# RWKV-7 and windowed attention block on one core: centred value tokens, row-tiled small products, unit product folded into the scores

## The reference, cut to what matters

```python
z = h @ w_in                                   # r, k, v, decay/rate/gate inputs, q, k, v, gates
w_log = -softplus(-(w0 + tanh(zw) @ w2)) - 0.5 # decay product, inner dimension 64
a = sigmoid(a0 + za @ a2)                      # rate product, inner dimension 64
# per head: S = S * w + (S aa) bb + v k ;  y = S r      (16 heads of 64)
mean = mean(y, axis=-1); var = mean(square(y - mean), axis=-1)
y = (y - mean) * rsqrt(var + GN_EPS) * lnx_w + lnx_b + bonus * v
s = q @ keys * 64 ** -0.5                      # chunks of 64 queries, 128 keys, softmax with a sink
```

## Time and profile before

| | |
|---|---|
| runs | 1233.83, 1238.17, 1239.98 us; median 1238.17 |
| profiled execution, own time | 1233.64 us |
| its span | 1232.0 us |
| mean granted TensorE clock | 0.988 |
| TensorE busy | 1147.1 us (93%) |
| VectorE, ScalarE, GpSimd busy | 655.6, 541.2, 92.3 us |
| weights loaded by SyncE's queue | 79.98 MB |

### The profile page before, as it was taken

How to read it: one execution, slowest core, us unless ns; L and a number is a source line. 1 busy time by engine, 2 the same in 40 slices (tenths; PEclk the granted TensorE clock), 3 DMA queues, 4 the chain that set the end, 5 groups by cost and what they waited for, 6 DMA issues and landing times. The chain is left out here.

```text
span 1232.0 us, 18748 instructions
## 1 busy us (share of the span) xinstructions
PE 1147.1 (93%) x7023; PEld 923.8 (75%) x7023; DVE 655.6 (53%) x1089; ACT 541.2 (44%) x991; POOL 92.3 (7%) x148
## 2 busy tenths in 40 slices
PE   4998999997989989999898799997999999999996
PEld 4887888885767767777677588885888888888785
DVE  4223545556667666676776444426566556553323
ACT  4435545554353443524544334335555464542222
POOL 8000000111011011010111001010000000000000
PEclk9999999999999999999999999998999999999998
DMA  8432232321011010110312245341323333322321
GB/s 209 103 86 86 60 103 78 90 82 35 10 53 44 10 53 9 44 44 10 104 40 71 74 134 156 112 125 57 95 86 101 98 89 97 90 88 86 91 81 73
DMA packets 171780, 97.23 MB, mean 79 GB/s; under 512 B 30873, under 2 KB 166727, under 8 KB 171719
## 3 DMA queue, kind: packets, MB, share of 16 engines
q1 hardware_dynamic: 166192, 79.98, 23.0%
q0 software_dynamic: 5376, 16.37, 4.4%
q10 hardware_dynamic: 151, 0.04, 0.0%
HBM read 87.98 MB, written 8.39 MB: 78 GB/s over the span
## 5 line engine op out<-in xcount | busy, mean ns | idle before, releaser
L1041 DVE TENSOR_TENSOR wlo<-raw,whi 128x1024 fp32r<-128x1024 f32 x148 | 181.2, 1225 | 335.0 <-ACT whi L667 335.0
L667 ACT ACTIVATE whi<-raw 128x1024 fp32r<-128x1024 f32 x148 | 156.2, 1057 | 264.0 <-PE ps L1533 262.8
L1528 PE MATMUL ps<-xnh,whi 128*128 128x512 f32 x352 | 140.4, 399 | 4.0 <-DVE xnl L1427 4.0
L1533 PE MATMUL ps<-xnh,wlo 128*128 128x512 f32 x352 | 139.6, 397 | 0.0
L1530 PE MATMUL ps<-xnl,whi 128*128 128x512 f32 x352 | 139.6, 397 | 0.0
L1528 PE MATMUL ps<-xh,whi 128*128 128x512 f32 x304 | 122.8, 404 | 0.0
L1533 PE MATMUL ps<-xh,wlo 128*128 128x512 f32 x304 | 120.2, 395 | 0.0
L1530 PE MATMUL ps<-xl,whi 128*128 128x512 f32 x304 | 120.1, 395 | 0.0
L1528 PEld LDWEIGHTS ps<-xnh,whi 128*128 128x128 f32 x352 | 66.5, 189 | 22.9 <-DVE xnl L1427 4.5
L1533 PEld LDWEIGHTS ps<-xnh,wlo 128*128 128x128 f32 x352 | 66.5, 189 | 15.9
L1530 PEld LDWEIGHTS ps<-xnl,whi 128*128 128x128 f32 x352 | 66.5, 189 | 15.4
(11 more groups left out here) (323 smaller groups left out, 2300.1 us busy)
## 6 DMA issues: line engine op xcount, KB each, us to landing
raw<-in_w_in SPq DMA_DIRECT2D x108, 256.0 KB, 3.2
raw<-in_w_up SPq DMA_DIRECT2D x88, 256.0 KB, 3.1
raw<-in_w_down SPq DMA_DIRECT2D x32, 256.0 KB, 2.9
gates_scratch<-gst POOLq DMA_DIRECT2D x16, 256.0 KB, 2.3
raw<-in_w_proj_a SPq DMA_DIRECT2D x16, 256.0 KB, 3.0
raw<-in_w_proj_b SPq DMA_DIRECT2D x16, 256.0 KB, 4.3
gl<-gates_scratch POOLq DMA_DIRECT2D x16, 256.0 KB, 3.8
raw<-in_w_out SPq DMA_DIRECT2D x16, 256.0 KB, 3.1
```

What stands on the lines that cost most here:

```text
L667: act.activation(flat(whi[:, hb]), flat(raw[:, b]), ACT.Copy).then_inc(w_hi, 1)
L1041: dve.tensor_tensor(flat(wlo[:, hb]), flat(raw[:, b]), flat(whi[:, hb]).bitcast(F32), ALU.subtract).then_inc(w_lo, 1)
L1528: pe.matmul(ps[bank][:, :], whi[:, hb, k, :], hi(k), start=first and k == 0, stop=False)
L1533: ins = pe.matmul(ps[bank][:, :], wlo[:, hb, k, :], hi(k), start=False, stop=last and k == kn - 1)
```

## The change

- Value tokens: the four transposes of v become four products with `centred` (unit matrix less the mean over each head), placed ahead of those of b and k and waiting for 7 masks instead of 8. `norm_mean` and `centre` go. ScalarE squares the scan's output directly and then copies it with the scale `lw`.
- The norm of the pair before moves: variance sums between the halves of the scores, deviations behind them, `scaled_output` ahead of the value tokens' copy, `with_bonus` at level 3; `gated` stays at level 5.
- Decay and rate products are two row tiles, 64 rows each, into two banks, issued together at the end of level 6 ahead of its filler step; the decay's tanh follows the key norms' copy.
- Attention scores are 8 products of 128 columns on 64 rows, alternating between the row halves and reading `kb` directly; the two `kc` copies per chunk go.
- `gb` gets -1 on its diagonal once, so that n1 carries the unit matrix, and the product with `nident16` in the remainder goes (8 per pair).

The diff, without declarations, semaphore lists and a few setup lines:

```diff
@@ -546,13 +538,13 @@
             diagonal(ident16, 1.0)
-            diagonal(nident16, -1.0)
             chain(pool.memset(eps_col[:, 1:2], 64e-5))
...
                     chain(pool.memset(t[h * HD:(h + 1) * HD, h * HD:(h + 1) * HD], value))
+            chain(pool.tensor_tensor(centred[:, :], ident[:, :], headmean[:, :], ALU.subtract))
@@ -605,9 +597,13 @@
                 attention_out(c)
-            pool.wait_ge(win_in, 8)
+            pool.wait_ge(scores_ps, 16)
             pool.wait_ge(vwin_in, 8)
-            pool.memset(gb[:, :, :, :], 0.0).then_inc(cleared, 1)
+            chain(pool.memset(gb[:, :, :, :], 0.0))
+            own = gb[:, :, :, 0:C].rearrange("p j h t -> p (j h) t")
+            pool.affine_select(out=own, in_=own, compare_op=ALU.not_equal, fill=-1.0, base=0,
+                               pattern=[[0, 2 * NT], [-1, C]], channel_multiplier=1)\
+                .then_inc(cleared, 1)
             for c in (6, 7):
@@ -734,10 +730,7 @@
                 act.activation(qc[:, :, :], q[:, :, bass.ds(c * AC, AC)], ACT.Copy,
-                               scale=HD ** -0.5)
-                act.activation(kc[0:HD, :, 0, :], kb[0:HD, :, bass.ds(c * AC, P)], ACT.Copy)
-                act.activation(kc[HD:P, :, 1, :], kb[HD:P, :, bass.ds(c * AC, P)], ACT.Copy)\
-                    .then_inc(win_in, 1)
+                               scale=HD ** -0.5).then_inc(win_in, 1)
@@ -793,13 +786,11 @@
-            def norm_head(d):
+            def norm_square(d):
                 act.wait_ge(out_ps, d + 1)
-                act.activation(ysb[:, :], ps[6][:, :], ACT.Copy).then_inc(y_copied, 1)
-
-            def norm_square(d):
-                act.wait_ge(yc_ready, d + 1)
-                act.activation(ysq[:, :], ysb[:, :], ACT.Square).then_inc(ysq_ready, 1)
+                act.activation(ysq[:, :], ps[6][:, :], ACT.Square).then_inc(ysq_ready, 1)
+                act.activation(ysb[:, :], ps[6][:, :], ACT.Copy, scale=pcol("lw", d))\
+                    .then_inc(y_scaled, 1)
@@ -853,8 +845,6 @@
                                        ACT.Copy).then_inc(y_ready[0], 1)
-                    if lv == 0 and d is not None:
-                        deviation(d)
                     if lv == 2:
@@ -863,10 +853,9 @@
                         gate_tile(2 * n)
-                    if lv == 5 and following:
-                        decay_tanh(n + 1)
                     if lv == 6 and following:
                         key_norm_back(n + 1)
+                        decay_tanh(n + 1)
                 transposed(LEVELS - 1)
@@ -931,9 +920,9 @@
                         hi_part(ybh, qb, i)
-                norm_head(n - 1)
+                norm_square(n - 1)
+                deviation(n - 1)
                 score_copy(n)
-                norm_square(n - 1)
                 gate_tile(2 * n - 1)
@@ -1082,10 +1070,10 @@
                 mask = notfirst[:, bass.ds(c * AC, P)].unsqueeze(1).to_broadcast([P, 4, P])
-                dve.wait_ge(scores_ps, c + 1)
-                for g in range(2):
-                    last = dve.tensor_tensor(sc[:, 4 * g:4 * g + 4, :],
-                                             ps[2 + g][:, :].rearrange("p (u k) -> p u k", k=P),
+                dve.wait_ge(scores_ps, 2 * c + 2)
+                for half in range(2):
+                    last = dve.tensor_tensor(sc[:, half:8:2, :],
+                                             ps[2 + half][:, :].rearrange("p (u k) -> p u k", k=P),
                                              mask, ALU.add)
@@ -1172,7 +1160,7 @@
                     dve.wait_ge(cleared, 3)
-                dve.wait_ge(tok_ps, n + 1)
+                dve.wait_ge(tok_ps, n * 3 + 1)
                 dve.tensor_copy(vp[:, :, 0:4:3, :],
@@ -1207,11 +1195,6 @@
-            def centre(d):
-                dve.wait_ge(mean_ps, d + 1)
-                dve.tensor_tensor(ysb[:, :], ysb[:, :], ps[4][:, :], ALU.subtract)\
-                    .then_inc(yc_ready, 1)
-
             def add_bonus(d):
@@ -1219,8 +1202,8 @@
                 dve.wait_ge(rstd_ps, d + 1)
-                chain(dve.scalar_tensor_tensor(ysb[:, :], ysb[:, :], pcol("lw", d), ps[4][:, :],
-                                               ALU.mult, ALU.mult))
+                dve.wait_ge(y_scaled, d + 1)
+                chain(dve.tensor_tensor(ysb[:, :], ysb[:, :], ps[4][:, :], ALU.mult))
@@ -1264,12 +1247,14 @@
                             .then_inc(y_ready[1], 1)
-                    if lv == 1 and d is not None:
-                        deviations(d)
+                    if lv == 2 and d is not None:
+                        add_bonus(d)
+                    if lv == 3 and d is not None:
+                        with_bonus(d)
                     if lv == 4 and following:
                         key_norms(n + 1)
-                    if lv >= 2 and lv < 6 and d is not None:
-                        (add_bonus, scaled_output, with_bonus, gated)[lv - 2](d)
+                    if lv == 5 and d is not None:
+                        gated(d)
                     if lv >= 4 and not following:
@@ -1358,17 +1343,17 @@
                     masked(n, f)
-                centre(n - 1)
+                deviations(n - 1)
                 for f in range(4, 8):
...
                 weights(N_GATE + 2 * n)
+                scaled_output(n - 1)
                 value_tokens(n)
...
                              lambda: y_lo(0, 0, 3), lambda: y_lo(0, 1, 4), lambda: y_lo(0, 2, 5)])
-            centre(PAIRS - 1)
             add_bonus(PAIRS - 1)
@@ -1566,13 +1551,14 @@
                 pe.wait_ge(win_in, c + 1)
-                for g in range(2):
-                    for ii in range(2):
-                        t = 4 * g + 2 * ii
-                        ins = pe.matmul(ps[2 + g][:, ii * 2 * P:(ii + 1) * 2 * P],
-                                        flat(qc[:, t:t + 2, :]), flat(kc[:, g, :, :]),
-                                        start=True, stop=True)
-                ins.then_inc(scores_ps, 1)
+                for t in range(0, 8, 2):
+                    for half in range(2):
+                        hs = slice(half * HD, (half + 1) * HD)
+                        ins = pe.matmul(ps[2 + half][:, t // 2 * P:(t // 2 + 1) * P],
+                                        qc[hs, t:t + 2, :].rearrange("p a b -> p (a b)"),
+                                        kb[hs, t // 4, c * AC:c * AC + P], start=True, stop=True)
+                        if t == 6:
+                            ins.then_inc(scores_ps, 1)
@@ -1584,13 +1570,12 @@
-            def decay_lora(n, bank=4):
-                pe.matmul(ps[bank][:, :], lora[:, n * P:(n + 1) * P], lora_w_in[:, :], start=True,
-                          stop=True).then_inc(lora_ps, 1)
-
-            def rate_lora(n, bank=5):
-                pe.matmul(ps[bank][:, :], lora[:, n * P:(n + 1) * P], lora_a_in[:, :], start=True,
-                          stop=True).then_inc(lora_ps, 1)
+            def small_products(n, banks=(4, 5)):
+                cols = slice(n * P, (n + 1) * P)
+                for h in range(2):
+                    hs = slice(h * HD, (h + 1) * HD)
+                    pe.matmul(ps[banks[h]][:, :], lora[hs, cols], lora_in[hs, :], start=True,
+                              stop=True).then_inc(lora_ps, 1)
@@ -1616,11 +1601,6 @@
                 turned(4, ysq).then_inc(rstd_ps, 1)
-
-            def norm_mean(d):
-                pe.wait_ge(y_copied, d + 1)
-                pe.matmul(ps[4][:, :], headmean[:, :], ysb[:, :], start=True, stop=True)\
-                    .then_inc(mean_ps, 1)
@@ -1644,9 +1624,9 @@
                     if f == 4:
+                        if d is not None:
+                            norm_var(d)
                         fill()
-                        if d is not None:
-                            norm_mean(d)
                     if f >= 4:
@@ -1658,11 +1638,16 @@
                 if d is not None:
-                    norm_var(d)
+                    deviations(d)
+                for j in range(NT):
+                    if j == 0:
+                        pe.wait_ge(g_ready, n * 8 + 7)
+                    ins = pe.matmul(ps[2][:, j * P:(j + 1) * P], z[:, n + 16, j * C:(j + 1) * C],
+                                    centred[:, :], start=True, stop=True)
+                ins.then_inc(tok_ps, 1)
                 pe.wait_ge(g_ready, n * 8 + 8)
-                for b, src in ((0, bp), (1, kp), (2, z[:, n + 16, :])):
-                    ins = turned(b, src)
-                ins.then_inc(tok_ps, 1)
+                for b, src in ((0, bp), (1, kp)):
+                    turned(b, src).then_inc(tok_ps, 1)
                 if d is not None:
@@ -1689,14 +1674,10 @@
-                    if lv == 2 and d is not None:
-                        deviations(d)
                     if lv == 3 and following:
...
                         gate(d)
-                    if lv == 5 and following:
-                        decay_lora(n + 1)
```

(37 more changed lines are left out.)

## The result

The changed kernel takes 1218.24 us (median of 4 runs, 1215.41 to 1221.17) against 1238.38 us before, a ratio of 0.984 with a 95% interval of [0.982, 0.987]. The forecast was 1218.0, with a range of 1209 to 1228. Both medians scatter: measured again later (e9), the same two kernels stood 17.9 us apart (1220.25 and 1238.18).

The account below looks back on a forecast made before the run. TensorE, busy 93% of the span, was taken as the bound; in the recurrence only where others wait for it. Terms sum to 21.3 us, less 2 for the clock: 19.3 off 1238.2, forecast 1218, range 1209 to 1228.

Parts of the forecast that it names:

- attention scores: Products of r, k and v: row-tiled scores take 1.07 us against 1.72 per chunk, seven chunks, 4.6 us off.
- decay and rate products ahead of pair 0: Dense part before the recurrence: both as two row tiles take 1.06 us instead of 1.86, 0.8 us off.
- middle pairs, six: Recurrence: each pair 1.9 us shorter, mostly at level 2 (0.95) and level 5 (0.75); 11.4 us off in all.
- pair 0: First pair of the recurrence, no norm work: masks start 0.85 us earlier; with remainder and tokens 1.2 us off.
- pair 7: Last pair of the recurrence, with no next pair: 0.95 + 0.7 + 0.15, 1.8 us off.
- tail: Last pair's serial norm ahead of the second projection: a wait and the mean product go, 1.5 us off.
- clock, and when the first rows land: Recurrence: one or two short falls of TensorE's clock, 2 us lost; the forecast sized no first-load term.
- rival D: More gain: pair 0's clock fall gets shorter and tiling switches cost less, 1209 to 1212 us; chance 0.07.
- rival A: VectorE becomes the bound at a pair's final decay scan and level 0: 4.5 us back, 1221 to 1225; chance 0.15.
- B: Short falls of the clock in most pairs, from a thinner stretch: 10 us back, 1226 to 1231; chance 0.10.
- E: Row tiles of 128 and 512 columns don't run together, in scores and decay/rate products: 1230 us; chance 0.03.
- C: Slower: levels 3 to 5 of seven later pairs fall to 1.2 GHz, 5.2 us each: 1253 us; chance 0.03.

Follow-up runs that it names:

- e9: The changed kernel with no edit, measured again beside the kernel before: 1220.25 us, 0.986 of before.
- e2: The changed kernel with the attention scores alone put back on all 128 rows, keys copied into a zero-padded block: 1220.89 us, 0.987 of before.
- e1: The changed kernel with each chunk's four score products of one row half ahead of the other half's, instead of alternating: 1224.06 us, 0.989 of before.
- e7: The changed kernel with the norm's later steps back at their old places, mean product still removed: 1240.52 us, 1.004 of before.
- e4: The changed kernel with VectorE's bonus add moved back from level 3 to behind the key norms of level 4: 1230.05 us.
- e6: The changed kernel with one more fp16 product per unit in the remainder, against zeros, replacing the removed unit product: 1225.19 us.
- e3: The changed kernel with the decay and rate products alone put back on all 128 rows at their old places: 1214.65 us.
- e5: The changed kernel with two extra VectorE operations of 0.43 us per pair ahead of the decay scan: 1225.07 us.

## Why the prediction was right

The mechanism was as forecast: the period came out, and of its parts the largest, the moves of the norm. That the total was right to 0.3 us is luck. Measured again, the changed kernel took 1220.25, 2.25 over the forecast, and stood 17.9 below the kernel before for the 20.1 of the first time; and errors of both signs lie in the sum. Term by term, measured from the traces and by taking parts back:

| term | forecast | measured | by |
|---|---|---|---|
| attention scores | 4.6 | 2.5 to 2.9 | spacing of chunks, e2 |
| decay and rate products ahead of pair 0 | 0.8 | 0.6 | key sums to key norms |
| middle pairs, six | 11.4 | 11.5 | period |
| pair 0 | 1.2 | 2.0, of which 1.0 to 1.2 is a shorter fall | scores to scan 0, e1 and e2 |
| pair 7 | 1.8 | 2.2 | scan 6 to scan 7 |
| tail | 1.5 | 1.8 | scan 7 to second projection |
| clock, and when the first rows land | -2 | -0.7 and -2.9 in the medians, -8.3 in the profiled pair | the two measurements; the three rises |

The terms but the last make 20.8 us with 2.7 for the scores, forecast 21.3. Against 20.1 and 17.9 between the medians that leaves 0.7 and 2.9 for the clock and the first loads, where 2 was set aside. In the two profiled executions they took 8.3: one pair of executions doesn't give this term.

**Pair 0: the size was there, in part for another reason.** Its fall is 10.2 us long before the change and 6.8 after it. In e1 and e2, which are the changed kernel from there on, it is 10.2 again, and the stretch from the first score product to scan 0 takes 33.3 and 33.1 us for the 34.1 of before. So the change itself gave 0.8 to 1.0 where 1.2 was forecast; the rest came with the shorter fall, which the forecast had only as rival D.

**Scores: mis-sized.** "8 slots of 0.109 and 0.2, so 1.07 us against 1.72: 0.65 less per chunk" took the switch from starts inside a row-tiled group and the start behind it. A switch also holds back the group's first record, which comes 0.20 behind the last transpose instead of 0.11, and the second record behind the group, 0.34 instead of 0.23. The group did take 1.09; the chunk gained 0.41. The same 0.2 is missing in the products ahead of pair 0: 0.6 for 0.8. So the term that was mis-sized is the price of a group's two switches, 0.2 in the prediction and 0.4 in the traces.

**A middle pair: 1.9 forecast, 1.92 measured, in other parts.** Moves of the norm: 0.95 at level 2 and 0.7 at level 5 forecast, 1.65 measured by e7, less its falls (1.73 in the last period, which had none), of it 0.77 for the bonus add by e4. Remainder: 0.25 forecast, 0.47 by e6; ScalarE's copies didn't hold the rest back, and the 0.45 counted in full. Products: "the level could have gone on only at 507.85 ... 0.4" was no gain. With the bonus add gone, the masks wait for the key norms, and the decay product ended under these. At level 6 the row tiles cost more than the 0.1 of the forecast, by the switch again. Together e3 finds a loss of 0.25 in the period. The mean product's removal is the rest: 1.92 - 1.65 - 0.47 + 0.25 leaves 0.05, as forecast, although it was the largest single product taken out. That is what is left over if the parts add up; no run takes this part back alone.

**What would show it.** Period 47.8: yes. Records in pairs: yes, in 1.1 us. Level 2 right behind its filler: yes (494.14 and 494.38, a filler's own distance). The update of level 5 waits 0.67 us, forecast "about 0.8". Clock full from 320 to 660: yes. VectorE's last sums: they still wait 0.3 us for TensorE, so rival A did not decide, by a third of a microsecond. Clearing gb: VectorE's maxima beside the clear take 679 to 691 ns, the last chunk's too, so the cost of 0 stands.

**The rivals.** B's mechanism exists: a middle pair half a microsecond longer, for any reason, showed it in two or three of six pairs (e4, e5, e6) and e7 in all. The forecast argued against it only by the full slices of before; what protects the changed kernel is thin, and the chance of 0.10 was no exaggeration. Why in e4 to e6 some pairs fall and others, with the same instructions, don't is not settled here. One hint: in e7 the six falls start 51.20 us apart, five times alike, while its scans are 50.85 to 51.14 apart, so that they drift from 39.9 to 40.7 us behind the scan. So the starts follow something other than the pair's own time, and when a pair comes may matter as well as what it does; no run tests that. E is out by the records in pairs, and for 512 columns by L1577: its four records start two by two, and the next product follows 1.06 us behind the first. C's size never came: a fall in a middle pair was 3.4 us long and cost 1.6. The half of D on pair 0's fall came, but in the profiled execution falls elsewhere took more than it gave.

## What to carry to other kernels

Cost a row-tiled group by the distance between two fixed points around it, not by its own records: here a pair of switches took 0.4 us, so 8 short products gained 0.41 of an expected 0.65, and the decay and rate products as two row tiles cost a pair 0.25 more than on all rows, where one of them fitted into a wait. Look for the wait first and then for the work: moving two filler steps into waits gave 1.35 us of each period, where the whole change gave 1.92, and kept the clock up besides. See for each wait which engine ended it: one of these two was a table load of ScalarE, not the masks. When a pipeline's pairs are compared, measure the period and list falls of the clock apart; totals of single runs differ by 6 us for the same period, and the gain between two medians was once 20.1 and once 17.9.

## What was not expected of the hardware

- A switch between full-height matmuls and row tiles costs 0.2 us in each direction, since neither side loads weights under the other: starts 0.20 and 0.34 us apart where 0.11 and 0.23 are usual. The page "TensorEngine Tiling (Array Packing)" of the Trainium skill, Key Properties, has the rule that a switch drains the engine; the traces agree, at twice what the prediction took from them.
- Row tiles ran together even where all products of one stood ahead of all of the other (e1): the second tile's first record started with the first tile's fifth of eight (189.77), ahead of three records that stand before it in the program.
- A fall of the clock for 3.4 us costs a middle pair 1.6 us and comes 39 to 41 us behind the scan (e4 to e7), where TensorE had been making short fp16 products with waits between; it comes and goes with changes of half a microsecond elsewhere in the pair.
